# Another order of the seven products of the second FFN matrix with one load for each sum, and another wait before the merge gate loads

## What is computed

```python
y = (g_f * y_f + g_p * y_p + g_m * y_m) @ w_out_l
x = x + gate1 * rms_norm(y, norm_g_l[1])
h = rms_norm(x, norm_g_l[2]) * (1 + scale2) + shift2
a, b = jnp.split(h @ w_ffn_in_l, 2, axis=-1)
x = x + gate2 * rms_norm((jax.nn.silu(a) * b) @ w_ffn_out_l, norm_g_l[3])
```

## Time and profile before

| | us |
|---|---|
| median of 3 runs | 1809.89 (1808.49 to 1811.78) |
| the profiled execution | 1809.75 |
| its span in the trace | 1807.9 |

### The profile page before, as it was taken

One profiled execution on the slowest core, in us unless ns is written; L12 is line 12 of the kernel. 1 busy time (PEld: TensorE's weight loads), 2 busy tenths in 40 slices (PEclk: granted clock), 3 DMA queues, 4 the chain that ended last, 5 costly groups with the idle time before them and its releaser, 6 DMA issues.

```text
span 1807.9 us, 24605 instructions
## 1 busy us (share of the span) xinstructions
PE 1732.9 (96%) x9622; PEld 1611.4 (89%) x9622; DVE 865.1 (48%) x1405; ACT 627.4 (35%) x1109; POOL 404.4 (22%) x476
## 2 busy tenths in 40 slices
PE   6999999999999999989989899999999999999996
PEld 3899998979999999987978799999999999887885
DVE  4400002333334444446867965444444443588885
ACT  6311113232222222223656483222222223454442
POOL 0400001322122232343415253222222220000000
PEclk9999999999999999989999999999999999999998
DMA  9544445654355556688758232222222225698683
GB/s 352 209 169 152 165 155 191 223 191 139 128 177 185 171 190 203 208 220 253 251 170 252 93 119 75 73 74 71 72 73 74 73 73 177 189 312 257 176 272 119
DMA packets 164266, 304.06 MB, mean 168 GB/s; under 512 B 13257, under 2 KB 98060, under 8 KB 164154
## 3 DMA queue, kind: packets, MB, share of 16 engines
q1 hardware_dynamic: 120288, 171.01, 29.5%
q0 software_dynamic: 27536, 91.31, 15.5%
q10 hardware_dynamic: 16336, 40.29, 6.7%
HBM read 234.79 MB, written 67.82 MB: 167 GB/s over the span
## 4 chain that ended last, share of the span: by engine, by line
PE 79%; DVE 6%; DMA 5%; ACT 3%; issue 3%; POOL 2%; SPq 2%; ACTq 0%; DVEq 0%; POOLq 0%
PE bank L658 24%; PE bank L659 24%; PE bank L660 24%; DMA raw<-in_w_stream 1%; DVE w_lo L1891 1%; PE bank L899 1%; DMA mg<-z_scratch 1%; PE bank L1144 1%; PE bank L1147 1%; PE bank L1154 1%; PE bank L1162 1%; DMA ada_raw<-in_w_ada 1%; SPq L753 1%; POOL ya L2705 1%; DMA z_scratch<-z_st 1%
## 5 line engine op out<-in xcount | busy, mean ns | idle before, releaser
L658 PE MATMUL bank<-h_hi,w_hi 128*128 128x384 f32 x1080 | 375.9, 348 | 7.8 <-DVE h_lo L2487 5.1
L659 PE MATMUL bank<-h_lo,w_hi 128*128 128x384 f32 x1080 | 365.8, 339 | 0.0
L660 PE MATMUL bank<-h_hi,w_lo 128*128 128x384 f32 x1080 | 365.5, 338 | 0.0
L1891 DVE TENSOR_TENSOR w_lo<-raw,w_hi 128x1024 fp32r<-128x1024 f32 x152 | 201.8, 1329 | 271.4 <-ACT w_hi L1414 270.9
L658 PEld LDWEIGHTS bank<-h_hi,w_hi 128*128 128x128 f32 x1080 | 204.1, 189 | 24.9 <-ACT z_st L1473 10.1
L1414 ACT CAST w_hi<-raw 128x1024 fp32r<-128x1024 f32 x152 | 157.4, 1050 | 169.4 <-DMA raw<-in_w_stream 107.4
L659 PEld LDWEIGHTS bank<-h_lo,w_hi 128*128 128x128 f32 x1080 | 204.4, 189 | 0.1
L660 PEld LDWEIGHTS bank<-h_hi,w_lo 128*128 128x128 f32 x1080 | 204.0, 189 | 0.0
L658 PE MATMUL bank<-w_hi,a_hi 128*128 128x512 f32 x352 | 139.6, 397 | 4.3 <-DVE w_lo L2382 4.3
L659 PE MATMUL bank<-w_lo,a_hi 128*128 128x512 f32 x352 | 140.6, 399 | 0.0
L660 PE MATMUL bank<-w_hi,a_lo 128*128 128x512 f32 x352 | 139.8, 397 | 0.0
(11 more groups left out here) (344 smaller groups left out, 3445.8 us busy)
## 6 DMA issues: line engine op xcount, KB each, us to landing
raw<-in_w_stream SPq DMA_DIRECT2D x142, 512.0 KB, 4.5
raw<-in_w_stream SPq DMA_DIRECT2D x101, 256.0 KB, 5.8
z_scratch<-z_st ACTq DMA_DIRECT2D x44, 576.0 KB, 3.1
raw<-in_w_ada SPq DMA_DIRECT2D x35, 512.0 KB, 5.7
a_raw<-f_scratch SPq DMA_DIRECT2D x44, 320.0 KB, 4.8
mg<-z_scratch ACTq DMA_DIRECT2D x24, 576.0 KB, 6.7
a_raw<-f_scratch SPq DMA_DIRECT2D x33, 256.0 KB, 5.1
zt<-z_scratch POOLq DMA_DIRECT2D x27, 256.0 KB, 3.6
```

The source lines that it names most:

```text
L658: pe.matmul(out, a_hi, b_hi, start=start, stop=False)
L659: pe.matmul(out, a_hi, b_lo, start=False, stop=False)
L660: return pe.matmul(out, a_lo, b_hi, start=False, stop=stop)
L1891: dve.tensor_tensor(w_lo[:, slot], raw[:, slot], w_hi[:, slot].bitcast(F32), ALU.subtract).then_inc(s_wlo, 1)
```

## The change

- The order of products is now (1, 7, 6, 5, 4, 2, 3), and `FO_TWO` holds 7 alone, and only for its weights. The A blocks of product 1 land in `S_ch` (640 columns wide now) and stay there, so that product 7 subtracts one newly loaded block from it in place. Products 6 and 5 need one A load and one weight load in a step. `a_aux` is gone, and T_ch, `ob` and `S_ch` lie at other places of SBUF.
- ACT copies the tiles of products 1 and 7 only. DVE takes out product 6 (`fo_u2`) and product 5 (`fo_u4`); `fo_rest` has two additions for a tile instead of three.
- The output tile `ALONE` is last. The sum of squares of its first half is made by ACT some steps before the end (`first_half_alone`), the second half has a square of 512 columns, and scaling and adding are done in two halves. The square writes into `T_ch` instead of `ob`; DVE, before its scaling, now waits for the store that used that half of `ob` two tiles earlier. The order on DVE at the end is scale, `fo_c12` of the next tile, add.
- In `e1(0)` `mg_load(x)` waits only for the store of the last of its own three rows; the waits on the stores of the mixer outputs stay. POOL's wait is not changed.

```diff
-FO_ORDER = (1, 7, 5, 6, 4, 2, 3)
+FO_ORDER = (1, 7, 6, 5, 4, 2, 3)
-FO_ASUM, FO_BSUM, FO_TWO = (7, 5, 6, 3), (7, 5, 6, 4), (7, 5)
+FO_ASUM, FO_BSUM, FO_TWO = (7, 6, 5, 3), (7, 6, 5, 4), (7,)
-FO_TILES = (5, 6, 7, 8, ALONE, 0, 1, 2, 3)
+FO_TILES = (5, 6, 7, 8, 0, 1, 2, 3, ALONE)
...
+                w = 640 if i in (1, 2, 3) else 512
+                dst = S_ch[:, k] if i == 1 else a_raw[:, s % AR, 0:w]
+                sp.dma_start(dst, f_dram[KF * rows + k, :, 640 * cols:640 * cols + w]).then_inc(s_al[s % AR], 16)
...
+                if 2 <= x < KT:
+                    z = Z1_UNITS + Z2_UNITS - KT + c
+                    act.wait_ge(s_zst[z % 2], 16 * (z // 2 + 1))
...
-                            act.wait_ge(s_zst[u], 8 * (Z_COUNT - 1))
...
+            def first_half_alone():
+                tile_done(act, FO_ORDER.index(2), 4)
+                act.activation(T_ch[:, 0], bank[6][:, :], ACT.Square, accum_out=stat[:, NT - 1, 0:1]).then_inc(s_ostat, 1)
...
-                    if k == KF - 1 and p < 3:
+                    if k == KF - 1 and p < 2:
                         for t in range(4):
                             fo_copy(p, t)
...
-                out, left, right, op = {7: (a, a, a_aux[:, x], ALU.subtract), 5: (ch, a, a_aux[:, x], ALU.add),
-                                        6: (ch, ch, a, ALU.subtract), 3: (a, a, ch, ALU.subtract)}[i]
+                out, left, right, op = {7: (ch, ch, a, ALU.subtract), 6: (ch, a, ch, ALU.subtract),
+                                        5: (a, ch, a, ALU.add), 3: (a, a, ch, ALU.subtract)}[i]
...
+            def fo_u2(t):
+                tile_done(dve, FO_ORDER.index(6), t)
+                dve.wait_ge(s_pact, OS + 8)
+                dve.tensor_tensor(R2[:, t, 0], R1[:, t, 0], fo_bank(2, t)[:, :], ALU.add).then_inc(s_pv, 1)
+
+            def fo_u4(t):
+                tile_done(dve, FO_ORDER.index(5), t)
+                dve.wait_ge(s_pv, V_U2 + t + 1)
+                dve.tensor_tensor(R1[:, t, 1], R2[:, t, 0], fo_bank(3, t)[:, :], ALU.add).then_inc(s_pv, 1)
...
-                o_out(len(OUT_AT))
-                for t in range(4):
-                    fo_c12(t)
-                    o_out(len(OUT_AT) + 1 + t)
+                fo_c12(0)
+                for t in range(4):
+                    o_scale(4 + t)
+                    if t < 3:
+                        fo_c12(t + 1)
+                    o_add(4 + t)
+                o_scale(NT - 1)
+                o_add(NT - 1)
```

More of the change, by code:

```diff
@@ L471, in build @@
         s_mxh, s_mxl = sem("mx_high"), sem("mx_low")
-        s_mg = [sem(f"merge_or_second_f_landed{i}") for i in range(MG)]
-        s_axl = s_mg
+        s_mg = [sem(f"merge_landed{i}") for i in range(MG)]
         s_ym, s_ya, s_yh, s_yl = (sem(n) for n in ("branches_gated", "y_summed", "y_high", "y_low"))
@@ L817, in b_load @@
                     second = e - 2 * RAW - fo_load(b, 0)
-                    if fo_product(b) not in (6, 4) and (fo_product(b), second) not in ((7, 0), (5, 1)):
+                    if fo_product(b) not in (6, 4) and (fo_product(b), second) != (7, 0):
                         sp.wait_ge(s_whi, split_index(U_FO) + fo_operand(b) + second + 1)
@@ L830, in a_load @@
                 i, k = fo_product(s), s % KF
-                rows, cols = FO_A[i][0]
+                rows, cols = FO_A[i]
                 if s == 0:
@@ L835, in a_load @@
                         sp.wait_ge(s_fs[g], 16 * PAIRS)
-                elif s >= AR:
+                elif s == KF:
+                    sp.wait_ge(s_fs[2], 16 * PAIRS)
+                if s >= AR:
                     step_done(sp, s - AR)
[L838 to L847, removed]
+                w = 640 if i in (1, 2, 3) else 512
+                dst = S_ch[:, k] if i == 1 else a_raw[:, s % AR, 0:w]
+                sp.dma_start(dst, f_dram[KF * rows + k, :, 640 * cols:640 * cols + w]).then_inc(s_al[s % AR], 16)
             def x1_load(r):
@@ L1867, in fo @@
                         o_square(SQUARE_AT.index(s))
+                    if s == FO_STEPS - 6:
+                        first_half_alone()
                 for r in range(len(SQUARE_AT), NT):
@@ L2424, in o_out, with o_add @@
                                          ALU.mult, ALU.mult).then_inc(s_oout, 1)
-                dve.wait_ge(s_oout, 3 * r + 2)
+            def o_add(r):
                 dve.wait_ge(s_x1l[r % 3], 16 * (r // 3 + 1 + (START_LOADS, 1, 1)[r % 3]))
-                for c in ((slice(0, D),) if r < NT - 1 else (slice(0, 512), slice(512, D))):
+                if FO_TILES[r] != ALONE:
+                    dve.wait_ge(s_oout, 3 * r + 2)
+                    dve.tensor_tensor(ob[:, r % 2], ob[:, r % 2], x1t[:, r % 3], ALU.add).then_inc(s_oout, 1)
+                    return
+                for half in range(2):
+                    c = slice(512 * half, 512 * half + 512)
+                    dve.scalar_tensor_tensor(ob[:, r % 2, c], bank[6 + half][:, :], stat[:, r, 5:6], G2bc[:, 0, c],
+                                             ALU.mult, ALU.mult).then_inc(s_oout, 1)
+                    dve.wait_ge(s_oout, 3 * r + 2 + 2 * half)
                     dve.tensor_tensor(ob[:, r % 2, c], ob[:, r % 2, c], x1t[:, r % 3, c], ALU.add).then_inc(s_oout, 1)
```

106 lines of the change are left out of this document (53 added, 53 removed).

## The result

Five executions of each kernel: 1799.71 us (1796.51 to 1804.28) after, 1809.89 us (1807.19 to 1811.91) before, a ratio of 0.9939 with a 95% interval of 0.9924 to 0.9955. That is 10 us less where 12.7 were predicted.

A forecast was written before the change was run, and what follows sets the result against it. TensorE was taken as the bound, busy 1732.9 of 1807.9 us, so only its waits, slow clock and tail could be gained: 1809.75 - 7.0 (`fo`) - 3.1 (end) - 2.6 (merge) = 1797.05, so 1797.0; range 1793.5 to 1803.0 us.

The forecast's parts named there:

- The loss in `fo`: Products 6 and 5 with two loads a step: TensorE no longer waits in `fo`, -7.0 us, bounds -4.3 and -7.0.
- the mean of 3.64 us: VectorE's step in old product 5, averaged over steps 24 to 31, against TensorE's 2.8 us a step.
- Product 7 and the moved evacuations: In `fo`, three loads instead of four in product 7, and evacuations moved from ACT to DVE: both priced at nothing.
- The cover: VectorE's lead in `fo` that hides the evacuations moved to it from TensorE: 4 to 5 us.
- The end: Work after TensorE's last matmul: last addition 4.0 us behind it instead of 7.3; -3.1 us taken, bounds -1.6 and -3.6.
- hidden by 0.6 us: At the end, tile r=6's store lands at about +0.6, before the last tile's scaling at +1.25; otherwise 1.5 us lost.
- The merge: Earlier gate load 2 lets unit 3's load land sooner, -1.8 us, and TensorE's clock stay higher, -0.8: together -2.6.
- The predicted sign: In the merge, TensorE waits for `mg` of unit 2 near 805 to 811, at unit 4 instead, some 6 us.
- The merge gives nothing: Rival: POOL's untouched wait ends last, so the merge gives nothing or costs; 1799.7 to 1801.2 us, chance 0.20.
- The loss moves: Rival: a smaller TensorE wait appears elsewhere in `fo`, with the lower clock again; 1800.5 to 1803.1 us, chance 0.10.
- it doesn't do what it says: Rival: transfers were not the bound in `fo`, VectorE's step stays 3.64 us, all 7.0 remain; 1804 to 1809, chance 0.06.
- slower: Rival: 3.64 us steps through products 6 and 5, VectorE held at each passage for PSUM; 1816.8 us, chance 0.04.

The follow-up runs named there:

- the last kernel: Changed kernel with POOL's sums of units 0 to 4 first, SP storing r = 5, 6 and 7, and output sums written into and stored from `x1t`: 1785.93 us, 0.9874.
- the pair on one chip: Changed kernel with its merge edit undone, beside the changed kernel itself on the same chip: 1802.07 us (0.9957) and 1799.32 us (0.9951).
- the idle work: Changed kernel with 5 extra VectorE additions where product 6 passes into 5 and 12 where 5 passes into 4; one traced execution, 1812.65 us.

## Why the prediction was right or wrong, point by point

*The loss in `fo`, -7.0: right, to the tenth.* 253.4 us became 246.4 with no wait and the full clock. The mechanism, bytes behind VectorE behind TensorE, held, but the prediction spread the cause over all four loads a step and only noted that `x1t` falls into the same stretch. The test with `x1t` alone moved gives it 5.3 of the 7.0. The term that was read too coarsely is the mean of 3.64 us: with 3.16 a step the lead nearly lasts to the end of the product, and it was the two steps of 4.45 us that emptied it. The 335 GB/s beside it counts what was issued; the DMA engines moved 311 GB/s from 1604 to 1640 us, which changes nothing in the sum. In the changed kernel the same three loads fell on steps with two loads. The prediction gave them 1 us of delay; VectorE's steps stayed at 2.41 us.

*Product 7 and the moved evacuations, nothing: right.* The cover was 5.7 us at the second passage, where 4 to 5 were given.

*The end, -3.1: wrong, 0.7 in the trace of after, and 0.3 to 0.7 in six other traces of kernels with this end and its stores on POOL.* The step that failed stands at the start of it: "The end: after TensorE's last matmul one more output tile is made serially." That chain, read from the earlier trace rows, was taken for the end of the program. The chain of waits ends at `DVEq L210` in those rows, 7.0 us before the span does, and the prediction did not ask what filled the rest. It was POOL's drain. The row that would have told was in the profile all along: POOL's and SP's instructions at L210. The sizes within the chain were nearly right: 7.3 to 4.66 us, for a forecast of 4.0. Of the 0.66 missed, 0.38 are VectorE's two waits for output stores (0.75 and 0.47 us), which made its last full tile late, so that the reciprocal started 1.55 us behind the last matmul and the scaling 1.79, not 1.25; without them it would be 4.3, by the last kernel. Half a scaling, which now reads its tile from PSUM, took 0.75 us, not 0.65. The prediction named this wait as hidden by 0.6 us and looked at one store only; the earlier one delayed the same chain.

*The merge, -2.6: open in the size, wrong in the account.* 3.3 us, within 2.6 either way, from four sets of times that were not all taken on one chip, but 1.1, within 3.7, from the pair on one chip, and nothing in nine traces. What was to bring it, gate load 3 landing up to 2.29 us earlier, did not happen: it took 9.9 us instead of 9.17, and `mg` of unit 3 came no earlier in any of the four traces with this edit alone. The step that failed is that traffic taken out of the crowded time would let this load land sooner, while POOL's wait held its issue where it was. The predicted sign that TensorE's wait shifts to the unit behind did: 5.06 us at 814.73. The longer wait at the end, 2.52 us at 833.90 in the earlier trace rows, was still there, 2.51 us at 838.27. The rule quoted from the Trainium skill ("DMA: Bandwidth & Descriptors", Queues, rings and completion order) agrees with the traces as far as they can be asked: the gate load put in right behind the last z store on the same queue did not push that store back (10.4 us to landing, 10.9 before), and gate load 3 gained nothing while the DMA engines were busy for 90% of the stretch.

*The rivals.* "The merge gives nothing" has its number, 1799.7, equal to the measured median, but that is luck: it takes the end at -3.1, and the end gave 2.4 us less. Two sums are left, and the runs do not decide between them. With the merge as forecast it is 1797.05 + 2.4 = 1799.5; with nothing from the merge it is 1809.75 - 7.0 - 0.7 = 1802.05, 2.3 us above the median, at the edge of what the times can tell. The rival's reason, POOL's untouched wait, is what the traces show: with that wait moved too, `mg` of unit 3 came 8 us earlier and the time fell by 4 us more. That 1799.7 lies inside the forecast does not speak for the terms of the end and the merge. "The loss moves", "it doesn't do what it says" and "slower" did not occur; the idle work shows how far the moved loss was, 5.7 us of VectorE's time.

## What to carry to other kernels

Before the tail of a kernel is shortened, subtract: the end of the span less the end of the last work in the chain. Where more than a fraction of a microsecond is left, look at every engine's closing instructions; here the program stayed open for 11.6 us from the issue of GpSimd's last store on, and moving two stores to another queue gave 4.3 us, where reworking the last tiles gave 0.7.

A mean step over a stretch hides the loads that do the damage. Print the steps one by one and see which are long; then move those loads before rewriting the order of products, since one line gave 5.3 of the 7.0 us.

Where two engines wait for the same event, list both waits. Taking one away can show little, as both edits by themselves did here, and is no proof that the event did not matter: both together gave 8.5 us.

## What the runs showed of the hardware

- GpSimd's drain at the end of the program took 8.23 us in every kernel in which it issued eight of the nine output stores, 8.07 with six of them and 7.99 with five. It began 0.2 to 0.3 us after its last store had landed: 3.1 us after the issue where the store took 2.9 us, 5.4 us after it where the store took 5.2. It ran beside everything else.
- A wait of 3.0 us of TensorE in `fo` was followed by a loss of 1.7 us, two of 2.54 and 1.73 us by 2.7 us; one of 1.47 us was not followed by any, with the granted clock at 1.00. In the merge the longest wait did not tell the granted clock of the 60 us: it was 0.97 with a longest wait of 2.6, 3.2 and 4.3 us, and 0.91 with 3.9, 4.1 and 5.1.
- The executions of one kernel lie 2 to 9 us apart, but for one outlier, and the faster ones are by and large those with the higher mean granted clock: 1796.5 us at 0.990 and 1804.3 at 0.984 in the changed kernel. In the profiled execution of the changed kernel it was low before 780 us (0.98, against 0.99), in stages that do not differ between the kernels. A trace of such an execution is compared stage by stage, never by its total.
